# S5's output matrices scaled later, and the experts' routing weights taken earlier

## The chip, the cores and the metric

The kernel runs on one NeuronCore of a Trainium2 chip, written directly against the engines: TensorE (PE), VectorE (DVE), ScalarE (ACT), GpSimd (POOL) and SyncE (SP) each have their own instruction stream, and they wait for each other by semaphores. The metric is the device time of one execution in microseconds (us). Before the change it is 2880.5 us, the median of three runs (2880.3 to 2881.02).

## The reference

One token sequence (256 tokens, width 1024, float32) goes through a first block and then through a second one of four layers.

```python
mod = silu(c) @ w_ada + b_ada                    # six modulation rows
h = x + gt1 * hybrid_mixer(modulate(rmsnorm(x), sh1, sc1))
h = h + gt2 * hier_moe(modulate(rmsnorm(h), sh2, sc2))

# hybrid_mixer: proj = a_in @ w_in, split into S5 (a linear recurrence with the
# output matrices c_re, c_im) and a gated delta rule; both joined by w_out
# S5: b_bar = ((lam_bar - 1) / lam) * b;  y = real(c . states) + d * u

# hier_moe: a token takes its best group of 4, and the best 2 of the group's 8 experts
w_k = softmax(top_val) * p_grp
out = sum over experts e of combine[:, e] * ((silu(hf @ wg[e]) * (hf @ wu[e])) @ wd[e])
```

The second block is attention or gated mixing between two feed-forward halves in each of four layers. The change doesn't touch it.

## The kernel before

Every large product is done in float32 by three matmuls of rounded parts: high times high, high times low, low times high. A weight slab of 128 x 2048 values is loaded by DMA, ACT copies it to its rounded high half (`slab_hi`, or `split_hi` in the first stages), and DVE subtracts to get the low half (`slab_lo`, `split_lo`). PE may use a slab once its low half stands. The order on each engine is written out by hand: each engine's function is a list of steps that run in just this order, so a step that waits holds everything behind it on that engine.

**The head.** PE multiplies eight slabs of `w_ada` (`ada_pe`, L1131), DVE takes each result out of PSUM (`ada_dve`, L1145 and L1154). There are two PSUM banks, so PE may begin slab j when slab j-2 has been taken out. GpSimd builds the tables of S5's rotations meanwhile, and DVE helps with the last two levels (`s5_table_dve`). `s5_c_dve` (L1273 to L1278) scales S5's output matrices `cx_re` and `cx_nim`, six operations of 128 x 512; it folds the factor (lam_bar - 1) / lam of the reference into c. It stands behind slab 0. PE needs its result only in `s5_pe`.

**The projections.** `w_in_pe`, `w_in_act` and `w_in_dve` work through ten slabs of `w_in`. ACT evacuates projection j and copies slab j+2's high half; DVE makes slab j+2's low half (L348) and, for j from 2 to 7, applies the convolution (L1344, L1346).

**The experts.** Tokens are sorted into five blocks of 128 slots: blocks 0, 1 and 2 for the groups in the order of their load, 3 and 4 for the largest one. The masks `mask(t, b)` pick tokens. `gather_pe` (L1838) brings a block's rows into PSUM with 32 matmul records, in two halves. `block_dve` modulates them (L1996), `block_hi_act` rounds them (L1949), and DVE makes their low half (L2001). There are 40 passes, one for an expert and a block. In pass n PE does `gate_up_pe` for the first half of the inner dimension, turns the hidden values of pass n-1 (`turn_h_pe`, L1880), does the second half, and then `down_pe` for pass n-1. Each half of `gate_up` and each `down` is a group of twelve 128 x 512 matmuls (L406 to L408). Two things are put into the first passes: `slot_weights_pe` (L1847), which brings the routing weights to the slots, and `turn_masks_pe` (L1856), which transposes the masks for the way back. `turn_masks_pe` waits until all five blocks have left PSUM; ACT copies the result (L1979, L1980), and `down_pe` of pass 3, the first that accumulates in the banks used for it, waits for these copies. The weights themselves are 21 small DVE steps (L2024 to L2083) with one exponential on ACT (L1962).

## Time and profile before

| | |
|---|---|
| median of 3 runs | 2880.5 us |
| profiled execution | 2873.54 us, span 2871.7 us |
| PE busy | 2752.7 us (96%) |
| DVE, ACT, POOL busy | 1597.9 (56%), 1233.0 (43%), 140.9 us (5%) |
| mean granted PE clock | 0.98 of full |
| HBM read | 506.04 MB, 177 GB/s over the span |

PE is busy for nearly the whole span, but a PE that is busy on a lower clock counts as busy too. So its idle times and the granted clock have to be read for single stretches. Times in rows are in us from the start of the span. A timeline row gives start, length, engine, line, operation, the count of merged instructions, and in brackets the idle time before it with what ended it. A name that ends in q is an engine's queue of issued DMAs. A float32 matmul of the modulation slabs shows as two records in the profile and one in the program's order, and so do the transposes and gathers.

### The profile page before, as it was taken

The numbers are of one execution on the slowest core, as the hardware profiler recorded it, in microseconds if no ns is written. First come the engines' busy times: TensorE is split into PE (matmuls) and PEld (weight loads), VectorE is DVE, ScalarE is ACT, GpSimd is POOL, SyncE is SP. The second block draws the span as 40 slices with busy tenths as digits, with TensorE's granted clock in tenths as the row PEclk, the third lists the DMA queues.
The fourth block names the chain that finished last, engine by engine and source line by source line (L and its number), as shares of the span: only waits on it lengthen the run. The fifth ranks groups of instructions, "written<-read, shape, count | busy, mean of one in ns | idle before, by whom it ended". The sixth has DMA issues, their size and how long they took to land. (4 is left out here: it accounts for less than half of the span.)

```text
span 2871.7 us, 35302 instructions
## 1 busy us (share of the span) xinstructions
PE 2752.7 (96%) x14506; PEld 2308.8 (80%) x14506; DVE 1597.9 (56%) x1821; ACT 1233.0 (43%) x1588; POOL 140.9 (5%) x227
## 2 busy tenths in 40 slices
PE   7988979999999999999998999999999999999998
PEld 6977877888788887888887888888878888896887
DVE  5884467767644536445455645545454464544544
ACT  3202245656534445344344434434453443444443
POOL 4000000000000100001000000000000010010000
PEclk9998989999999999999999999999999999999999
DMA  7432056878655544656553755554435556452652
GB/s 249 156 108 88 30 200 229 310 279 297 220 181 176 167 138 136 207 189 213 193 166 107 240 182 176 191 187 153 144 118 183 195 178 206 155 169 90 225 176 88
DMA packets 349485, 509.35 MB, mean 177 GB/s; under 512 B 14880, under 2 KB 295488, under 8 KB 349328
## 3 DMA queue, kind: packets, MB, share of 16 engines
q1 hardware_dynamic: 342960, 484.17, 49.9%
q0 software_dynamic: 5792, 20.78, 2.1%
q8 instruction: 112, 1.84, 0.3%
q10 hardware_dynamic: 576, 2.20, 0.2%
q14 instruction: 45, 0.37, 0.0%
HBM read 506.04 MB, written 1.05 MB: 177 GB/s over the span
## 5 line engine op out<-in xcount | busy, mean ns | idle before, releaser
L393 DVE TENSOR_TENSOR raw_r<-raw,whi 128x2048 fp32r<-128x2048 f32 x185 | 421.9, 2290 | 170.3 <-ACT whi L385 169.3
L833 ACT ACTIVATE h_hi<-psum 128x256 fp32r<-128x256 f32 x216 | 82.8, 383 | 758.5 <-PE psum L772 684.2
L385 ACT ACTIVATE whi<-raw 128x2048 fp32r<-128x2048 f32 x185 | 351.1, 1909 | 12.4 <-DMA raw<-in_w_up 6.7
L888 DVE TENSOR_TENSOR h_lo<-psum,h_hi 128x256 fp32r<-128x256 f32 x216 | 91.5, 424 | 437.1 <-ACT h_hi L833 437.1
L407 PE MATMUL psum<-place_lo,act_hi 128*128 128x512 f32 (+1 forms) x840 | 318.6, 379 | 0.0
L406 PE MATMUL psum<-whi,act_hi 128*128 128x512 f32 (+1 forms) x872 | 308.2, 353 | 5.4 <-DVE act_lo L639 4.3
L408 PE MATMUL psum<-whi,act_lo 128*128 128x512 f32 (+1 forms) x872 | 302.1, 346 | 0.0
L393 DVE TENSOR_TENSOR place_lo<-arena,place_hi 128x2048 fp32r<-128x2048 f32 x107 | 244.2, 2289 | 91.8 <-ACT place_hi L385 91.8
L407 PE MATMUL psum<-raw_r,act_hi 128*128 128x512 f32 (+1 forms) x808 | 283.8, 351 | 0.0
L406 PE MATMUL psum<-place_hi,act_hi 128*128 128x512 f32 (+1 forms) x592 | 234.1, 395 | 0.0
L408 PE MATMUL psum<-place_hi,act_lo 128*128 128x512 f32 (+1 forms) x592 | 228.6, 386 | 0.0
L406 PE MATMUL psum<-wlo,act_hi 128*128 128x512 f32 (+1 forms) x520 | 192.4, 370 | 13.4 <-DVE act_lo L639 9.5
L385 ACT ACTIVATE place_hi<-arena 128x2048 fp32r<-128x2048 f32 x107 | 202.9, 1908 | 1.3 <-DMA arena<-in_ff_w_in 1.3
L408 PE MATMUL psum<-wlo,act_lo 128*128 128x512 f32 (+1 forms) x520 | 187.4, 360 | 0.0
L406 PEld LDWEIGHTS psum<-whi,act_hi 128*128 128x128 f32 x872 | 165.7, 190 | 24.7 <-issue 4.8
L408 PEld LDWEIGHTS psum<-whi,act_lo 128*128 128x128 f32 x872 | 165.7, 190 | 21.0
L407 PEld LDWEIGHTS psum<-place_lo,act_hi 128*128 128x128 f32 x840 | 158.0, 188 | 29.1
L393 DVE TENSOR_TENSOR wlo<-wlo_f,wlo 128x2048 fp32r<-128x2048 f32 x61 | 139.7, 2290 | 73.2 <-ACT wlo L385 72.3
L407 PEld LDWEIGHTS psum<-raw_r,act_hi 128*128 128x128 f32 x808 | 153.7, 190 | 18.5
L826 ACT ACTIVATE scratch<-psum 128x256 f32<-128x256 f32 x216 | 82.1, 380 | 188.2 <-PE psum L408 188.2
L406 PE MATMUL psum<-act_hi,whi 128*128 128x256 f32 x496 | 142.4, 287 | 8.1 <-DVE act_lo L601 5.9
L407 PE MATMUL psum<-raw_r,h_hi 128*128 128x512 f32 x372 | 145.4, 391 | 0.0
(537 smaller groups left out, 5832.7 us busy)
## 6 DMA issues: line engine op xcount, KB each, us to landing
arena<-in_ff_w_in SPq DMA_DIRECT2D x182, 512.0 KB, 4.9
raw<-in_ff_w_in SPq DMA_DIRECT2D x126, 512.0 KB, 4.9
arena<-in_ff_w_out SPq DMA_DIRECT2D x88, 512.0 KB, 4.5
raw<-in_ff_w_out SPq DMA_DIRECT2D x68, 512.0 KB, 4.5
wlo_f<-in_ff_w_in SPq DMA_DIRECT2D x44, 512.0 KB, 4.9
raw<-in_w_ada SPq DMA_DIRECT2D x20, 1024.0 KB, 5.2
raw<-in_w_gate SPq DMA_DIRECT2D x35, 512.0 KB, 4.4
raw<-in_w_up SPq DMA_DIRECT2D x35, 512.0 KB, 5.4
```

The costliest lines, as they stand in the source:

```text
L385: act.activation(hi, loaded, ACT.Copy).then_inc(S("slab_hi"), 1)
L393: dve.tensor_tensor(lo, loaded, hi.bitcast(F32), ALU.subtract).then_inc(S("slab_lo"), 1)
L406: pe.matmul(out_ap, lhs[0], rhs[0], start=first, stop=False)
L407: pe.matmul(out_ap, lhs[0], rhs[1], start=False, stop=False)
L408: return pe.matmul(out_ap, lhs[1], rhs[0], start=False, stop=last)
L826: act.activation(pair_of(sil, g), gate_up(g)[:, 0:256], ACT.Silu).then_inc(S("pass_sil"), 1)
L833: act.activation(pair_of(turned_h[0], g), gate_up(g)[:, 0:256], ACT.Copy).then_inc(S("pass_turned_hi"), 1)
L888: dve.tensor_tensor(pair_of(turned_h[1], g), gate_up(g)[:, 0:256], pair_of(turned_h[0], g).bitcast(F32), ALU.subtract)\
```

## The change

Three steps are moved; no arithmetic is added or taken away.

1. `s5_c_dve` leaves the place behind modulation slab 0 and stands in `w_in_dve` behind the low half made at j = 1, which is that of the fourth slab (index 3). The counts of its semaphore change places with those of the tables.
2. The routing weights: `slot_weights_pe` moves ahead of the third gather and of the second half of pass 0. On DVE the weights' steps move ahead of block 0's low halves and of the first two expert slabs; `block_dve` is cut so that its two halves stand between them. On ACT the pair's exponential and the change to SiLU's table move ahead of block 0.
3. `turn_masks_pe` and ACT's copies of its result move from pass 3 to pass 4.

```diff
-S5_DVE = {..., "s5_c": (11,), "table_im": (12, 13),
+S5_DVE = {..., "table_im": (11, 12), "s5_c": (13,),
...
             for j in range(10):
                 next_lo(dve, "w_in", j, 10)
+                if j == 1:
+                    s5_c_dve(dve, done)
...
                 if n:
                     turn_h_pe(pe, n - 1)
+                if n == 0:
+                    slot_weights_pe(pe)
                 if n < 3:
                     gather_pe(pe, n + 2)
-                elif n == 3:
+                elif n == 4:
                     turn_masks_pe(pe)
                 gate_up_pe(pe, n, 1)
                 if n:
                     down_pe(pe, n - 1)
-                else:
-                    slot_weights_pe(pe)
...
             act.activation(gexp, gexp, ACT.Exp).then_inc(S("group_exp"), 1)
+            act.wait_ge(S("pair_diff"), 1)
+            act.activation(pair_e, pair_e, ACT.Exp).then_inc(S("pair_exp"), 1)
+            act.activation(warm, warm, ACT.Silu)
             block_hi_act(act, 0)
             slab_hi(act, "moe", 0)
             slab_hi(act, "moe", 1)
-            act.wait_ge(S("pair_diff"), 1)
-            act.activation(pair_e, pair_e, ACT.Exp).then_inc(S("pair_exp"), 1)
-            act.activation(warm, warm, ACT.Silu)
...
-                if n == 3:
+                if n == 4:
                     act.wait_ge(S("moe_turned_raw"), 1)
...
-            block_dve(dve, 0)
-            slab_lo(dve, "moe", 0)
-            slab_lo(dve, "moe", 1)
...
             dve.tensor_tensor(pair_e, m2, m1, ALU.subtract).then_inc(S("pair_diff"), 1)
+            block_dve(dve, 0, 0)
             dve.wait_ge(S("group_exp"), 1)
             done(dve.reduce_sum(gden, by(gexp, 4), AX))
             done(dve.reciprocal(gden, gden))
+            block_dve(dve, 0, 1)
             dve.wait_ge(S("pair_exp"), 1)
...
             dve.tensor_tensor(oh1, oh1, oh2, ALU.add).then_inc(S("moe_weights"), 1)
+            block_lo_dve(dve, 0)
+            slab_lo(dve, "moe", 0)
+            slab_lo(dve, "moe", 1)
             dve.wait_ge(S("moe_slot_raw"), 1)
...
                 if n < 4:
-                    block_dve(dve, n + 1)
+                    block_dve(dve, n + 1, 0)
+                    block_dve(dve, n + 1, 1)
+                    block_lo_dve(dve, n + 1)
...
                 ada_dve(dve, done, j)
-                if j == 0:
-                    s5_c_dve(dve, done)
-                elif j in (2, 4):
+                if j in (2, 4):
                     s5_table_dve(dve, done, TABLE_SHARED + j // 2 - 1)
```

In the orders below `arena`, `scratch`, `small` and `diag` are SBUF tiles and `cols` holds the matrices c. This is DVE's order in the projections before: the low halves of slabs 2, 3 and 4, and the first convolution.

```order
L1331 MEMSET scratch 128x2x3 x2
L348 TENSOR_TENSOR wlo<-raw,whi 128x2048 x3
L1344 TENSOR_SCALAR arena<-scratch,cols 128x256 x2
L1346 SCALAR_TENSOR_TENSOR arena<-scratch,cols,arena 128x256 x6
L348 TENSOR_TENSOR wlo<-raw,whi 128x2048
```

And this is the same place now.

```order
L1331 MEMSET scratch 128x2x3 x2
L348 TENSOR_TENSOR wlo<-raw,whi 128x2048 x2
L1273 TENSOR_TENSOR arena<-cols,small 128x512
L1274 TENSOR_TENSOR arena<-cols,small 128x512
L1275 TENSOR_TENSOR cols<-cols,small 128x512
L1276 TENSOR_TENSOR cols<-cols,small 128x512
L1277 TENSOR_TENSOR cols<-cols,arena 128x512
L1278 SCALAR_TENSOR_TENSOR cols<-cols,arena 128x512
L348 TENSOR_TENSOR wlo<-raw,whi 128x2048
L1346 TENSOR_SCALAR arena<-scratch,cols 128x256 x2
L1348 SCALAR_TENSOR_TENSOR arena<-scratch,cols,arena 128x256 x6
```

The six operations now stand between the low halves of slab 3 and slab 4.

DVE's order at the start of the experts before: the last masks, block 0, the first two expert slabs (L393), and only then the weights, of which the first two steps and the last one are shown with what follows them.

```order
L2063 TENSOR_SCALAR scratch<-arena,small 128x128 x4
L1996 TENSOR_SCALAR act_f<-psum,modc 128x128 x8
L2001 TENSOR_TENSOR blocks_r<-act_f,blocks_r 128x512 x2
L393 TENSOR_TENSOR raw_r<-raw,whi 128x2048 x2
L2024 TENSOR_REDUCE small<-small 128x2
L2025 TENSOR_TENSOR small<-small 128x16
...
L2083 TENSOR_TENSOR small<-small 128x16
L2085 COPY small<-psum 128x40
L393 TENSOR_TENSOR raw_r<-raw,whi 128x2048
```

Now, from the last of the first twelve steps of the weights on:

```order
L2072 TENSOR_TENSOR small<-small 128x2
L1996 TENSOR_SCALAR act_f<-psum,modc 128x128 x4
L2075 TENSOR_REDUCE small<-small 128x2
L2076 RECIPROCAL small<-small 128x2
L1996 TENSOR_SCALAR act_f<-psum,modc 128x128 x4
L2079 TENSOR_SCALAR small<-small 128x2
...
L2085 TENSOR_TENSOR small<-small 128x16
L2004 TENSOR_TENSOR blocks_r<-act_f,blocks_r 128x512 x2
L393 TENSOR_TENSOR raw_r<-raw,whi 128x2048 x2
L2090 COPY small<-psum 128x40
L393 TENSOR_TENSOR raw_r<-raw,whi 128x2048
```

All steps of the weights now stand ahead of the first slabs, and the copy of the slots' weights out of PSUM stands behind the first two slabs as it did.

PE's order in pass 0 before, from the last matmul of the first half on: the gather, the second half, the slots' weights.

```order
L408 MATMUL psum<-whi,blocks_r 128x512
L1838 MATMUL psum<-diag,arena 128x128 x16
L406 MATMUL psum<-whi,blocks_r 128x512
...
L408 MATMUL psum<-whi,blocks_r 128x512
L1847 MATMUL psum<-small,scratch 128x8 x8
L1847 MATMUL psum<-small,diag 128x8 x2
L406 MATMUL psum<-whi,blocks_r 128x512
```

Now:

```order
L408 MATMUL psum<-whi,blocks_r 128x512
L1849 MATMUL psum<-small,scratch 128x8 x8
L1849 MATMUL psum<-small,diag 128x8 x2
L1840 MATMUL psum<-diag,arena 128x128 x16
L406 MATMUL psum<-whi,blocks_r 128x512
```

The ten small matmuls have moved ahead of the gather and of the twelve matmuls of the second half. The ten mask transposes (L1856, now L1858) have moved by one pass, behind the turn of pass 3's hidden values.

## Rows read from the trace of the kernel before

**Rows 1.** Windows: length, busy PE, PEld, DVE, ACT, POOL, granted clock, DMA share, GB/s.

```profile
460.00:740.00 280.00, 280.00 (x1242) 226.42 (x1241) 206.30 (x147) 170.90 (x146) 0.00 (x0) 1.00 0.82 295
27.00:29.00 2.00, 2.00 (x6) 1.60 (x5) 1.97 (x3) 0.00 (x0) 1.40 (x1) 0.54 1.09 365
```

**Rows 2.** Waits of PE, whole kernel: us in total, times, longest.

```profile
PE psum L406 <- DVE raw_r L393: 5.8, 2, 3.2
...
PE psum L1856 <- DVE act_f L1996: 5.7, 1, 5.7
```

**Rows 3.** Timeline of PE, 0 to 48 us: start, length, what, idle before.

```profile
9.49 13.41 PE L1131 MATMUL psum<-raw,small 128*128 128x256 f32 x48 [9.49 <-DMA raw<-in_w_ada]
25.30 5.38 PE L1131 MATMUL psum<-act_f,small 128*128 128x256 f32 x16 [2.40 <-DVE diag L1145]
...
40.88 3.62 PE L1131 MATMUL psum<-raw,small 128*128 128x256 f32 x16
```

**Rows 4.** Timeline of DVE, 18 to 25 us.

```profile
19.40 1.10 DVE L1274 TENSOR_TENSOR arena<-cols,small 128x512 f32<-128x512 f32 x1
```

**Rows 5.** Issue of the eighth modulation slab, on the SP queue.

```profile
23.91 1.18 SPq L1116 DMA_DIRECT2D raw<-in_w_ada  x1
```

**Rows 6.** DMA issued from 23.9 to 25 us: KB, us to landing.

```profile
raw<-in_w_ada SPq DMA_DIRECT2D x1, 1024.0 KB, 11.8
```

**Rows 7.** Timeline of DVE, 60 to 125 us.

```profile
70.63 2.29 DVE L348 TENSOR_TENSOR wlo<-raw,whi 128x2048 fp32r<-128x2048 f32 x1 [3.47 <-ACT whi L343]
76.39 2.29 DVE L348 TENSOR_TENSOR wlo<-raw,whi 128x2048 fp32r<-128x2048 f32 x1 [3.47 <-ACT whi L343]
...
82.15 2.29 DVE L348 TENSOR_TENSOR wlo<-raw,whi 128x2048 fp32r<-128x2048 f32 x1 [0.19 <-ACT whi L343]
...
121.53 0.69 DVE L1415 TENSOR_TENSOR arena<-psum,arena 128x512 f32<-128x512 f32 x1 [2.53 <-PE psum L1375]
```

**Rows 8.** Timeline of ACT, 79 to 80 us.

```profile
79.72 0.60 ACT L1323 ACTIVATE scratch<-psum 128x512 f32<-128x512 f32 x1 [3.36 <-PE psum L408]
```

**Rows 9.** Timeline of DVE, 383 to 445 us.

```profile
383.81 1.37 DVE L1996 TENSOR_SCALAR act_f<-psum,modc 128x128 f32<-128x128 f32 x4 [2.31 <-PE psum L1838]
...
389.99 2.29 DVE L393 TENSOR_TENSOR raw_r<-raw,whi 128x2048 fp32r<-128x2048 f32 x1 [1.55 <-ACT whi L385]
...
404.02 0.20 DVE L2085 COPY small<-psum 128x40 f32<-128x40 f32 x1 [5.10 <-PE psum L1847]
...
412.62 0.47 DVE L2011 SCALAR_TENSOR_TENSOR scratch<-scratch,small,psum 128x256 f32<-128x256 f32 x1
...
441.00 0.42 DVE L888 TENSOR_TENSOR h_lo<-psum,h_hi 128x256 fp32r<-128x256 f32 x1
```

**Rows 10.** Timeline of PE, 395 to 470 us.

```profile
395.32 3.73 PE L1838 MATMUL psum<-diag,arena 128*128 128x128 f32 x32
...
401.69 1.85 PE L1847 MATMUL psum<-small,scratch 128*128 128x8 f32 x16
...
406.61 0.80 PE L406 MATMUL psum<-whi,blocks_r 128*128 128x512 f32 x1 [2.62 <-DVE raw_r L393]
...
413.14 0.44 PE L1880 MATMUL psum<-mats,scratch 128*128 128x128 f32 x2 [1.43 <-DVE scratch L2011]
...
444.02 1.97 PE L1856 MATMUL psum<-mats,scratch 128*128 128x128 f32 x8 [5.73 <-DVE act_f L1996]
...
464.33 0.38 PE L1880 MATMUL psum<-mats,scratch 128*128 128x128 f32 x2
```

**Rows 11.** Timeline of ACT, 397 to 448 us.

```profile
397.44 1.28 ACT L1963 ACT_TABLE_LOAD   x1
...
444.00 0.63 ACT L1949 ACTIVATE blocks_r<-act_f 128x512 fp32r<-128x512 f32 x1 [0.65 <-DVE act_f L1996]
446.46 1.02 ACT L1979 ACTIVATE turned_r<-psum 128x1024 fp32r<-128x1024 f32 x1 [1.82 <-PE psum L1856]
```

**Rows 12.** Page, costliest groups: busy, mean ns, idle before.

```profile
L385 ACT ACTIVATE whi<-raw 128x2048 fp32r<-128x2048 f32 x185 | 351.1, 1909 | 12.4 <-DMA raw<-in_w_up 6.7
```

More of the change, by code:

```diff
@@ L91 @@
 S5_ACT = {"c_act": (1,), "s5_step": (2,), "s5_rad": (3,), "s5_turn": (4, 5)}
-S5_DVE = {"half": (1,), "s5_lr": (2,), "s5_angle": (3,), "turn_pow": (4, 5, 6, 7, 8, 9, 10), "s5_c": (11,), "table_im": (12, 13),
+S5_DVE = {"half": (1,), "s5_lr": (2,), "s5_angle": (3,), "turn_pow": (4, 5, 6, 7, 8, 9, 10), "table_im": (11, 12), "s5_c": (13,),
           "s5_last": (14, 15, 16, 17)}
@@ L1988, in moe_act, with block_dve, block_lo_dve @@
             slab_hi(act, "ff0a", FF_HEAD[1])
-        def block_dve(dve, q):
-            b = BLOCK_ORDER[q]
-            for half in range(2):
-                dve.wait_ge(S("moe_gathered"), 2 * q + half + 1)
-                for c in range(4):
-                    k = 4 * half + c
-                    last = dve.tensor_scalar(mod_part(q, half)[:, c * P:(c + 1) * P], gathered(q, half)[:, c * P:(c + 1) * P],
-                                             modc[:, 3, k:k + 1], modc[:, 2, k:k + 1], ALU.mult, ALU.add)
-                last.then_inc(S("moe_block_f"), 1)
+        def block_dve(dve, q, half):
+            dve.wait_ge(S("moe_gathered"), 2 * q + half + 1)
+            for c in range(4):
+                k = 4 * half + c
+                last = dve.tensor_scalar(mod_part(q, half)[:, c * P:(c + 1) * P], gathered(q, half)[:, c * P:(c + 1) * P],
+                                         modc[:, 3, k:k + 1], modc[:, 2, k:k + 1], ALU.mult, ALU.add)
+            last.then_inc(S("moe_block_f"), 1)
+        def block_lo_dve(dve, q):
+            b = BLOCK_ORDER[q]
             for half in range(2):
```

## The prediction

> **What bounds the kernel now.** I read the windows first. In the expert passes PE is busy for all of 280.00 us at full clock, while DVE is busy 206.30 and ACT 170.90 [rows 1]. So there nothing is gained by relieving DVE or ACT; only time in which PE stands still, or runs at its lower clock, can be won. The list of PE's waits comes next: it is short, and the change touches three places in it. Two waits on a low half of a slab come to 5.8 us and one on the blocks' rows to 5.7 us [rows 2]; the third, 2.40 us on DVE among the modulation slabs, is in PE's timeline [rows 3]. I then read the timelines of PE, DVE and ACT round each place, to see what was queued ahead of what ended the wait.
>
> **Part one, S5's output matrices (`s5_c_dve`).** Six DVE operations leave the place behind the first modulation slab. There they hold DVE while PE has finished the third slab (9.49 + 13.41 = 22.90) and waits for the second's evacuation until 25.30 [rows 3]. Behind the wait the fourth slab takes 5.38 us where the eighth takes 3.62 [rows 3], because the granted clock had fallen to its lower level: it averages 0.54 from 27 to 29 us [rows 1], 1.2 GHz for nearly all of it. Without the six, DVE evacuates at once. The gain is the wait, 2.40, plus the slow slab, 5.38 - 3.62 = 1.76: 4.2 us.
>
> Is something else late then? The eighth slab is issued at 23.91 [rows 5] and lands 11.8 us later [rows 6], at 35.7. PE wants it at 22.90 + 4 x 3.5 = 36.9 (3.5 is a slab's 3.62 less the drain of its last matmul, which overlaps the next slab). That leaves a second. DVE's two table parts and its evacuations fit between PE's slabs, since PE asks only for the evacuation of the slab before the last. What follows the eighth slab (the scaling of the rows, the first projection) hangs on PE's and DVE's end of it, and moves forward by the same 4.2.
>
> The six operations now stand behind the fourth projection slab's low half. That split starts at 70.63 and ends at 72.92; the next starts at 76.39 after 3.47 us idle [rows 7]. The six are 128x512 each. Their price from two sides: beside GpSimd's table operations one took 1.10 [rows 4], with the chain 6.0 us in all if each did; a 128x512 operation with GpSimd idle took 0.69 [rows 7], which with a drain behind every second comes to 4.0 us. GpSimd's timeline is empty from 60 to 110 us, so I take 4.0. DVE is then free at 76.9 in place of 76.39, and the fifth slab's low half is ready at 79.15. PE wants it when the fourth slab ends, which is when ACT evacuates it, at 79.72 [rows 8]. So 0.5 us of cover remains, cost nothing. From then on DVE's idle time before a split is 0.19 [rows 7], by which the lateness melts slab by slab. With 6.0 the low half would come at 81.2, 1.5 us late, once.
>
> By the Trainium skill ("SBUF — State Buffer", section "Who interferes with whom") a DVE instruction with two SBUF inputs contends with a GpSimd instruction that reads SBUF; that is these operations at their old place, and the trace agrees (1.10 against 0.69 [rows 4, 7]). By that rule the price at the new place is the lower one.
>
> **Part two, the routing weights.** Before, DVE runs 21 small steps for the weights behind the first two expert slabs' splits, PE does its small products for them (`slot_weights_pe`) last in pass 0, at 401.69, and DVE waits 5.10 us for them until 404.02 [rows 9, 10] before it may split the second expert's first slab. PE then stands still 2.62 us until 406.61 and again 1.43 us until 413.14 [rows 10], and its matmuls between these are the slow ones. The change puts the small products ahead of the third gather: PE reaches them at 395.32 [rows 10], if the weights are ready. DVE's wait ends 401.69 - 395.32 = 6.37 us sooner. From there to the end of pass 0's hidden values (412.62) DVE has no wait [rows 9], so that whole run moves by 6.37. ACT must follow: its splits of the second expert's two slabs no longer stand behind the pair's exponential, and the slabs are loaded early. PE: gather and second half end near 404.0, the next half is ready for it, 2.8 us at full clock ends at 406.8, and the turn of pass 0 waits until 406.8 in place of 413.14. Gain 6.4 us. DVE bounds the rounds of passes 1 and 2, which keep their length.
>
> Are the weights ready at 395.32? The 21 steps take 4.2 us. They now fill DVE's idle stretches: 2.31 ahead of the first half block, 0.51 between its halves, 1.55 ahead of the first slab's low half at 389.99 [rows 9], 4.4 us together. They end at about 388.5, seven us early, and the first slab's low half is not late. On ACT a table load of 1.28 us [rows 11] moves ahead of the first block's copy; it starts at 384.1, when the pair's difference is there, and ends with the copy of one element at 385.6, where the half block is ready at 385.2 [rows 9]. 0.4 us late, behind which ACT waits for a DMA until 388.05 anyway. Cost nothing.
>
> The Trainium skill ("ScalarE: Activation LUTs", section "What ACT_TABLE_LOAD costs") speaks against this: 2.66 us for each switch of set, a drain of about 1.38 included. The row shows 1.28 and the next instruction right behind [rows 11]. By the rule the two half-block copies would end near 388.2 and the first slab's split start 0.1 us late: the sum would be smaller by 0.1.
>
> **Part three, the masks' turn.** In pass 3 PE stands still 5.73 us, from 438.29, because turning the masks waits for all ten half blocks; the turn at 444.02 and the half pass behind it run on the lower clock [rows 10]. From 438.29 to the turn of pass 4's hidden values at 464.33 [rows 10] it is 26.0 us. Now the same stretch is, at 2.8 us for a group of twelve 128x512 matmuls (280.00 / 1242 = 0.225 us each [rows 1], and a little for the step between groups): half pass 2.8; the product down of pass 2 waits for its low half, ready at 441.42 [rows 9], so it starts at 3.2 and ends at 6.0; half pass 8.8; turn 9.1; ten mask turns at full clock 1.4, to 10.5; half pass 13.3. Then down of pass 3 needs ACT's copies of the turned masks. ACT's queue: second half block until 444.63 [rows 11], which is 6.3 in this count; SiLU 0.3; three slab copies of 1.9 [rows 12] and one of 0.3; mask copies 1.02 [rows 11] and 0.3: 13.9. PE waits 0.6, starts down at 14.0, ends 16.8, half pass 19.6. Gain 26.0 - 19.6 = 6.4 us. Then PE is bound by itself again [rows 1] and keeps the lead.
>
> **The sum.** 4.2 + 6.4 + 6.4 = 17.0 us. The profiled execution took 2873.54 us (span 2871.7), the median of the runs is 2880.5, 7 us more; the saved stretches are alike in both, so I take them off the median: 2863.5 us, 0.6% faster. Against the profiled execution it would be 2856.5.
>
> **The rivals.**
> 1. The projections pay: DVE's six operations take 6.0 us, the fifth slab is 1.5 us late. For it: DVE has 5.6 us of work in every 5.76 us there. Against: GpSimd idle. Time 2865.0.
> 2. The head gains nothing, since the modulation slabs are bound by their DMAs: the margin of the eighth slab is only a second, and the DMA engines are full there (share 1.09, 365 GB/s [rows 1]). Against: loads land in the order of their issue and at 365 GB/s a slab takes 2.9 us, so each earlier slab has landed at least that much earlier than the one behind it, while PE wants them 3.5 apart. Time 2880.5 - 12.8 = 2867.7.
> 3. The masks' gain is given back: in pass 4 ACT holds the copies of the masks behind two slab copies, each of which waits for its DMA; PE's product down of pass 3 waits for them. If these slabs land 6.4 us behind need, 2869.9. Against: their places are given free by pass 2 and pass 1, over ten us earlier.
> 4. Slower: the same mechanism without a bound. The wait for the masks now hangs on two loads where before it hung on DVE alone. It decides from the point where the two slabs are ready 17 us behind PE's need; at 25 us the price is 25 less 17.0, 2888.5. A slab of 1024 KB landed in 11.8 us even in the fullest stretch [rows 6], so I hold this for nearly excluded.
> 5. That the change doesn't do what it says (the order of the engines' instructions shows all three moves) or is undone by a later stage, 2880.5.
>
> **How the numbers follow.** Forecast 0.76, rival 1 0.06, 2 0.07, 3 0.06, 4 0.02, 5 0.03. The range reaches to 2869.5 above, to take in rivals 1 and 2 and part of 3, and to 2858 below, since PE may find more of its lower clock gone than I count. A measurement of this kernel tells 0.2%, 5.8 us, from no change: faster is the forecast and rivals 1 to 3, 0.95; same 0.03; slower 0.02.
>
> **What would show it.** PE's modulation slabs in one run from 9.5 to 40.3 us at full clock. DVE's split of the fifth projection slab at 76.9 and no wait of PE behind it. The small products of the slots at about 391 (all stages here 4.2 earlier), no wait of PE for `raw_r` behind them, and only one of the two 5.8 us left, the 3.2 in front of the first slab. No 5.7 us wait in pass 3, the mask turns in pass 4, and a wait under 1 us for ACT's copies. The forecast is wrong if the eighth slab's end has moved by less than 3 us, if PE waits in the projections, or if the turn of pass 4 comes later than 448.5.

## The result, and the profile after

The changed kernel took 2862.1 us (median of 4 runs, 2858.9 to 2866.8), the kernel before 2880.4 us (4 runs, 2878.0 to 2881.0). The ratio on record is 0.9947, with an interval of 0.9933 to 0.9961: faster by 0.53%, 11.2 to 19.3 us. It is an estimate of its own and not the quotient of the two medians, which is 0.9936. The forecast was 2863.5. The profiled execution of the changed kernel took 2859.13 us (span 2857.3), that of before 2873.54 (span 2871.7).

Read the new profile in the same order. First the windows, of the changed kernel: the head from 24 to 29 us, and the expert passes that the change touches (length, busy time of PE, PEld, DVE, ACT and POOL with instructions, granted clock, DMA share, GB/s):

```profile
24.00:29.00 5.00, 5.00 (x25) 4.41 (x24) 4.49 (x5) 0.00 (x0) 3.48 (x3) 1.00 1.10 356
380.00:452.00 72.00, 67.82 (x383) 57.13 (x382) 60.02 (x86) 42.53 (x42) 0.00 (x0) 1.00 0.71 258
```

The same windows in the kernel before:

```profile
24.00:29.00 5.00, 3.70 (x9) 3.00 (x10) 4.83 (x8) 0.00 (x0) 4.18 (x4) 0.66 1.09 355
380.00:452.00 72.00, 59.01 (x325) 51.03 (x326) 51.93 (x98) 32.64 (x34) 0.00 (x0) 0.88 0.56 205
```

The clock went from 0.66 to 1.00 in the head and from 0.88 to 1.00 in the passes, and PE is busy for 67.8 of 72 us instead of 59.0. Of PE's waits in [rows 2], one of the two on `raw_r` (now 3.3 us, once) and the one on `act_f` are gone.

PE in the head of the changed kernel, from the fourth slab (start, length, engine, line, operation, tiles, count, idle before and what ended it):

```profile
22.61 3.62 PE L1131 MATMUL psum<-act_f,small 128*128 128x256 f32 x16
26.06 3.62 PE L1131 MATMUL psum<-scratch,small 128*128 128x256 f32 x16
...
37.86 3.69 PE L1131 MATMUL psum<-raw,small 128*128 128x256 f32 x16 [1.28 <-DVE diag L1145]
43.20 1.94 PE L546 MATMUL psum<-mats,scratch 128*128 128x128 f32 x16 [1.66 <-DVE scratch L586]
```

Against [rows 3] the wait of 2.40 us ahead of the fourth slab and the slow slab are gone, as forecast. The 1.28 us ahead of the eighth slab are new, and it is DVE's evacuation that ends them, not a DMA. What DVE and GpSimd did then, first DVE, then GpSimd (POOL):

```profile
30.70 2.00 DVE L1245 TENSOR_TENSOR arena<-arena,gain_row 128x1024 f32<-128x1024 f32 x1
32.62 3.38 DVE L1246 TENSOR_TENSOR arena<-arena,gain_row 128x1024 f32<-128x1024 f32 x1
36.03 1.23 DVE L1247 TENSOR_TENSOR arena<-arena 128x1024 f32<-128x1024 f32 x1
37.29 0.42 DVE L1145 TENSOR_TENSOR diag<-psum,mats 128x256 f32<-128x256 f32 x1
31.69 3.22 POOL L1247 TENSOR_TENSOR arena<-arena 128x1024 f32<-128x1024 f32 x1
```

The same stretch of the kernel before, DVE and then GpSimd:

```profile
35.15 1.97 DVE L1245 TENSOR_TENSOR arena<-arena,gain_row 128x1024 f32<-128x1024 f32 x1
37.05 1.21 DVE L1246 TENSOR_TENSOR arena<-arena,gain_row 128x1024 f32<-128x1024 f32 x1
33.69 2.35 POOL L1247 TENSOR_TENSOR arena<-arena 128x1024 f32<-128x1024 f32 x1
```

Read what lies beside what. Before, GpSimd's last operation ended at 36.04, under the first of DVE's three, and the other two (the first of them is shown) took 1.2 us each. Now DVE's three begin 4.45 us earlier and GpSimd's only 2.00, so DVE's L1246, from 32.62 on, lies beside 2.3 of the 3.2 us of GpSimd's L1247 (until 34.91) and takes 3.38 in place of 1.21. The three take 6.6 us instead of 4.4, and PE waits for the evacuation queued behind them. The eighth slab's load was no longer far off either: issued at 24.20 and 11.8 us under way, it landed at 36.0, 0.4 us before PE would have started on it (two slabs, 6.9 us, behind 29.51). The forecast had a margin of a second.

In the projections of the changed kernel, the first and the last of the six operations behind the fourth slab's split, and the next split on DVE:

```profile
69.43 0.69 DVE L1273 TENSOR_TENSOR arena<-cols,small 128x512 f32<-128x512 f32 x1
72.70 0.69 DVE L1278 SCALAR_TENSOR_TENSOR cols<-cols,arena 128x512 f32<-128x512 f32 x1
73.30 2.28 DVE L348 TENSOR_TENSOR wlo<-raw,whi 128x2048 fp32r<-128x2048 f32 x1
```

The six cost 0.69 each and 3.9 us in all (69.43 to 73.30), and the low half is ready at 75.58. PE has no wait there.

PE in pass 0 of the changed kernel, from the first expert product to the turn of its hidden values; below it the DVE copy that waits for the small products:

```profile
388.49 0.47 PE L406 MATMUL psum<-whi,blocks_r 128*128 128x512 f32 x1 [3.33 <-DVE raw_r L393]
391.38 1.85 PE L1849 MATMUL psum<-small,scratch 128*128 128x8 f32 x16
393.52 3.82 PE L1840 MATMUL psum<-diag,arena 128*128 128x128 f32 x32
...
402.83 0.44 PE L1882 MATMUL psum<-mats,scratch 128*128 128x128 f32 x2
393.70 0.20 DVE L2090 COPY small<-psum 128x40 f32<-128x40 f32 x1 [2.75 <-PE psum L1849]
```

The two waits of 2.62 and 1.43 us in [rows 10] are gone, and DVE waits 2.75 us where it waited 5.10 [rows 9]. PE at the masks, now in pass 4, and the first of ACT's two copies of them, with the turn of pass 4's hidden values at 447.25 (it stood at 464.33 [rows 10]):

```profile
431.15 0.51 PE L406 MATMUL psum<-wlo,h_hi 128*128 128x512 f32 x1 [0.37 <-DVE h_lo L888]
437.07 1.03 PE L1858 MATMUL psum<-mats,scratch 128*128 128x128 f32 x8
441.60 0.47 PE L406 MATMUL psum<-act_hi,h_hi 128*128 128x512 f32 x1 [0.47 <-ACT turned_r L1982]
447.25 0.38 PE L1882 MATMUL psum<-mats,scratch 128*128 128x128 f32 x2
440.15 1.03 ACT L1981 ACTIVATE turned_r<-psum 128x1024 fp32r<-128x1024 f32 x1
```

Pass 3 has only the wait of 0.37 us that was forecast, eight of the ten mask turns take 1.03 us at full clock (1.97 before [rows 10]), and ACT's copies make PE wait 0.47.

The same points of the program in both traces, in us:

| point | before | after | lead |
|---|---|---|---|
| transposes of the weights begin (L546) | 46.15 | 43.20 | 2.95 |
| router's result copied on DVE | 374.74 | 370.63 | 4.11 |
| first expert product (L406) | 392.43 | 388.49 | 3.94 |
| turn of pass 0's hidden values | 413.14 | 402.83 | 10.31 |
| turn of pass 2's | 437.85 | 427.54 | 10.31 |
| turn of pass 4's | 464.33 | 447.25 | 17.08 |
| end of the span | 2871.7 | 2857.3 | 14.4 |

### The profile page after: what moved, and what is told of

Read it like the earlier page. It is cut to its first block and busy times, and to the rows that moved or that the text cites. A ratio compares the mean times of both kernels' runs of the same rounds, so it can differ in the third digit from the quotient of the medians.

```text
span 2857.3 us, 35303 instructions
## 1 busy us (share of the span) xinstructions
PE 2749.0 (96%) x14506; PEld 2305.6 (81%) x14506; DVE 1597.7 (56%) x1821; ACT 1233.5 (43%) x1588; POOL 138.2 (5%) x227
## 5 line engine op out<-in xcount | busy, mean ns | idle before, releaser
L393 DVE TENSOR_TENSOR raw_r<-raw,whi 128x2048 fp32r<-128x2048 f32 x185 | 421.8, 2290 | 168.0 <-ACT whi L385 167.2
L406 PE MATMUL psum<-whi,act_hi 128*128 128x512 f32 (+1 forms) x872 | 308.7, 354 | 5.4 <-DVE act_lo L639 4.3
L393 DVE TENSOR_TENSOR place_lo<-arena,place_hi 128x2048 fp32r<-128x2048 f32 x107 | 244.2, 2290 | 90.7 <-ACT place_hi L385 90.7
L406 PE MATMUL psum<-place_hi,act_hi 128*128 128x512 f32 (+1 forms) x592 | 234.1, 395 | 0.0
L406 PE MATMUL psum<-wlo,act_hi 128*128 128x512 f32 (+1 forms) x520 | 192.5, 370 | 13.4 <-DVE act_lo L639 9.5
L406 PEld LDWEIGHTS psum<-whi,act_hi 128*128 128x128 f32 x872 | 166.4, 191 | 24.8 <-issue 4.8
L393 DVE TENSOR_TENSOR wlo<-wlo_f,wlo 128x2048 fp32r<-128x2048 f32 x61 | 139.7, 2290 | 74.4 <-ACT wlo L385 73.7
L406 PE MATMUL psum<-act_hi,whi 128*128 128x256 f32 x496 | 142.1, 286 | 8.1 <-DVE act_lo L601 5.9
```

Source lines behind the costliest of these rows:

```text
L393: dve.tensor_tensor(lo, loaded, hi.bitcast(F32), ALU.subtract).then_inc(S("slab_lo"), 1)
L406: pe.matmul(out_ap, lhs[0], rhs[0], start=first, stop=False)
```

## Experiments

Lengths between near points of this table are used below, since they hang less on what happened earlier in a run than times from its start do. Each experiment's kernel, the changed one and the one before had one execution profiled; two kernels were profiled a second time, as experiments of their own. The ratios below compare with runs of the kernel before from the same batch, whose medians were 2879.8, 2878.9 and 2881.9 us. In the largest batch, 24 runs of the kernel before, single runs took 2871.5 to 2886.1 us.

**The first part alone.** The kernel before with `s5_c_dve` at its new place.

```
- if j == 0: s5_c_dve(dve, done)          # behind the first modulation slab
- elif j in (2, 4): s5_table_dve(...)
+ if j in (2, 4): s5_table_dve(...)
+ if j == 1: s5_c_dve(dve, done)          # in the loop over the projection slabs
```

> Part one alone: the scaling of S5's output matrices behind the fourth projection slab, the rest as before. Theory (the parts add): in the trace the end of the eighth modulation slab comes 3 us earlier than before, the router's first copy on DVE about 4 us earlier, the turns of passes 0 and 4 keep their distance from it; time 2877 us, 0.1% faster. Rival (the head's gain is lost in the projections or in the S5 stage): the router's first copy within 1 us of 374.7. Either way DVE's second table part beside GpSimd makes PE wait about 1.3 us ahead of the eighth slab.

Measured: 2871.7 us, ratio 0.9979 (0.9967 to 0.9992). The transposes begin at 43.12, 3.0 us earlier than before, with the same new wait on PE:

```profile
37.77 3.69 PE L1131 MATMUL psum<-raw,small 128*128 128x256 f32 x16 [1.48 <-DVE diag L1145]
```

The new wait stands by itself, without the other parts. The size of the gain is less firm than one pair says. The head with its old order was profiled in two more kernels, those of the second and of the third part alone. PE's fourth slab, in the first and then in the second of them:

```profile
25.85 5.38 PE L1131 MATMUL psum<-act_f,small 128*128 128x256 f32 x16 [3.16 <-DVE diag L1145]
26.80 5.38 PE L1131 MATMUL psum<-act_f,small 128*128 128x256 f32 x16 [3.62 <-DVE diag L1145]
```

The wait that was 2.40 us in the kernel before is 3.16 and 3.62 there, and the transposes begin at 46.69 and 47.64 instead of 46.15. With the new order they begin at 42.96 to 43.53 in seven profiled executions, and the new wait is 0.62 to 1.48. So the move brings 2.6 to 4.7 us, by which old head and which new one are compared; 3.0 is the pair of the first two profiles. Two more readings differ from what was expected. The router's result comes 5.7 us earlier than before, not 4, as the stretch from the transposes to it took 2.7 us less. And the turn of pass 0 lies 40.2 us behind it, not 38.4, since PE ran at its low clock behind the first expert product.

**The second part alone.** The kernel before with the weights and the small products at their new places.

```
- else: slot_weights_pe(pe)               # last in pass 0
+ if n == 0: slot_weights_pe(pe)          # ahead of the gather
  (with ACT's pair exponential and DVE's weight steps as in the change)
```

> Part two alone: the routing weights early, the masks turned in pass 3 and the S5 scaling in its old place. Theory (the slots' weights end a wait of DVE): DVE's wait for the slots' weights ends 6.4 us earlier than before, measured from the router's first copy (22.9 us behind it in place of 29.3), and so does the turn of pass 0 (32.0 in place of 38.4); PE waits once, not twice, for a low half; time 2874 us. Rival (the granted clock, not the wait, carries the gain, and it depends on what else the stage does): the turn of pass 0 gains less than 5 us.

Measured: 2872.7 us, ratio 0.998 (0.9968 to 0.9992). From the first expert product to the turn of pass 0 it takes 15.90 us, against 20.71 before and 14.34 in the changed kernel. The gain of 4.8 us (4.5 from the router's copy on, 38.4 before and 33.9 now) is under the 5 us that the rival named. But PE waits once for a low half and not twice, as the theory said, and the missing 1.56 us are clock, not order: PE's window behind the first product, of this kernel and then of the changed one, differs in the column of the granted clock:

```profile
388.00:402.00 14.00, 11.50 (x70) 10.39 (x71) 9.27 (x6) 5.76 (x4) 0.00 (x0) 0.88 0.88 355
```
```profile
386.00:400.00 14.00, 11.51 (x77) 10.45 (x78) 10.85 (x11) 6.01 (x5) 0.00 (x0) 1.00 0.89 356
```

The same two lengths come in the other kernels. With the small products ahead of the gather the stretch took 14.3 in four profiled executions and 15.9 in five; with them at the old place 20.7 in two and 22.27 in the one of the first part alone (clock 0.88 from 386 to 400 us). Within one clock the gain is 20.71 - 14.34 = 6.37 and 22.27 - 15.90 = 6.37: the forecast's term to the digit. So the rival is right that the clock moves the length, by 1.56 us from one execution to another, and wrong that it carries the gain.

**The third part alone.** The kernel before with the masks' turn in pass 4.

```
- elif n == 3: turn_masks_pe(pe)
+ elif n == 4: turn_masks_pe(pe)
- if n == 3: act.wait_ge(S("moe_turned_raw"), 1) ...
+ if n == 4: act.wait_ge(S("moe_turned_raw"), 1) ...
```

> Part three alone: the masks turned in pass 4. Theory: from the turn of pass 2 to the turn of pass 4 it takes 19.7 us in place of 26.5, as in the changed kernel; the start of the experts is as before; time 2873.6 us. Rival (the gain needs the lead in loads that part two gives): ACT's copies of slabs in pass 4 wait for DMAs, the distance is over 22 us and the time above 2876.

Measured: 2870.7 us, ratio 0.9976 (0.996 to 0.9992). From the turn of pass 2 to that of pass 4 it takes 19.67 us, in the changed kernel 19.71 and before 26.48. In its new place the turn makes the stretch 19.4 to 19.7 us long in every profile but one (18.75, see below). The old order's 26.48 is less steady. With the first part alone the stretch took 25.68, with the second alone 27.00, and the cause can be read: the wait ends 6.17 us behind the turn of pass 2 in all three, but the low clock behind it lasts for 2, 6 and 8 of the expert matmuls (0.54 us and more each, where 0.40 is full clock). So the part brings 6.8 us against the kernel before, and 6.0 to 7.3 by how long PE stays at the low clock there. No slab copy of ACT waited for a DMA, so the gain doesn't need the second part's lead. The three ratios alone give 0.21, 0.20 and 0.24%, 0.65% together, where the whole has 0.53% and, measured again below, 0.56%. The parts add up within what the intervals leave open.

**The small products behind the gather.** The changed kernel with its first part and third part whole, and the small products one place later.

```
+ if n < 3: gather_pe(pe, n + 2)
  if n == 0: slot_weights_pe(pe)
- if n < 3: gather_pe(pe, n + 2)
```

> The changed kernel, but PE's small products for the slots' weights stand behind the third gather instead of ahead of it, so half of the move is undone. Theory (DVE's run behind the slots' weights bounds the start, so the gain is what PE does behind them): the gather's 3.5 us come back in full at the turn of pass 0 (35.5 us behind the router's first copy in place of 32.2), time 3.5 us above the changed kernel. Rival (PE bounds the run by now): less than 1.5 us comes back.

Measured: 2868.1 us, ratio 0.9954 (0.9936 to 0.9972). From the first product to the turn of pass 0 it takes 19.44 us, 5.1 more than in the changed kernel. PE shows the gather's 3.6 us ahead of the small products, and the half pass behind them partly at 0.63 us for a matmul where full clock gives 0.40:

```profile
397.12 3.73 PE L1840 MATMUL psum<-diag,arena 128*128 128x128 f32 x32
400.69 1.85 PE L1849 MATMUL psum<-small,scratch 128*128 128x8 f32 x16
404.75 0.63 PE L406 MATMUL psum<-whi,blocks_r 128*128 128x512 f32 x1
412.14 0.44 PE L1882 MATMUL psum<-mats,scratch 128*128 128x128 f32 x2 [1.89 <-DVE scratch L2016]
```

Against the runs that have the same low clock behind the first product (15.90) the stretch is 3.54 us longer, one gather. So DVE's wait for the small products is what the run of pass 0 hangs on: moved by a gather, it moves by a gather. The rest of the 5.1, 1.56, is clock.

**Three more operations in the projections.** The changed kernel with three 128x512 operations on DVE behind the six.

```
  if j == 1:
      s5_c_dve(dve, done)
+     for _ in range(3): done(dve.tensor_tensor(arena[128x512], mats, mats, ALU.add))
```

> The changed kernel with three more DVE operations of 128x512 behind S5's six in the projections (work that nothing needs), 2.1 us in all. Theory (the place has 0.7 us of cover: in the changed kernel the fifth slab's low half ends at 75.58, PE wants it at 76.31): the fifth slab's low half is 1.4 us late, PE waits 1.4 us once, ahead of the fifth slab, and the later slabs wait for nothing or for little. Rival (the lateness is paid anew at each slab, since DVE has only 0.2 us to spare in each): PE waits in total over 3 us in the projections.

Measured: 2862.7 us, one run. ACT's evacuations of the projections show the price, and that it is paid once: the distance is 5.76 us up to the evacuation at 76.26, 7.63 to the next, and 5.76 again from there on (89.65); the last line is PE's wait:

```profile
76.26 0.60 ACT L1323 ACTIVATE scratch<-psum 128x512 f32<-128x512 f32 x1 [3.36 <-PE psum L408]
83.89 0.60 ACT L1323 ACTIVATE scratch<-psum 128x512 f32<-128x512 f32 x1 [5.23 <-PE psum L408]
77.84 0.38 PE L406 MATMUL psum<-act_hi,whi 128*128 128x256 f32 x1 [1.62 <-DVE wlo L348]
```

The three take 2.13 us and PE waits 1.62 (1.4 was expected), so by the wait 0.5 us of cover was left, the forecast's figure. ACT's next evacuation comes 1.87 late. Of the 0.25 between, 0.16 is the end of a matmul that the next one otherwise overlaps, and 0.09 the slower first matmul behind the wait (0.38 in place of 0.28 us). Past the edge only the difference is paid, once. A single run's time can't show 1.9 us; the trace does.

**The masks back in pass 3, with the wait filled.** The changed kernel with the masks' turn at its old place, and matmuls of no use ahead of it, so that PE is busy while it waits. First with 44 of them.

```
- elif n == 4: turn_masks_pe(pe)
+ elif n == 3:
+     keep_clock(pe, 5, 44)      # second kernel: 24
+     turn_masks_pe(pe)
```

> The changed kernel with the masks' turn back in pass 3, and 44 small matmuls of the unit matrix into a free bank in front of it, which fill PE's wait of 5.7 us. It splits the 6.8 us of the masks' part into wait and clock. Theory (most of it is the wait, a third the clock): PE stays at full clock through the stretch, the ten mask turns take 1.2 us in place of 2.4 and the half pass behind them 2.8 in place of 3.9, so that from the turn of pass 2 to the turn of pass 4 it takes 24.2 us, between 26.5 (masks in pass 3) and 19.7 (in pass 4). Rival (the slow clock is all of it, PE would have waited later anyway): under 21.5 us.

The filler was mis-sized. The 44 matmuls took 9.8 us, 0.22 each, longer than the wait of 5.73 that they were to fill, and the stretch from the turn of pass 2 to that of pass 4 was 28.17 us, which neither theory had. So it was run again with 24.

> The masks' turns back in the pass where they were, with 24 matmuls of no use (their results are not read) ahead of them instead of the 44 that had overshot: at 0.22 us each they take about 5.3 us, less than the wait of 5.7 us that stood there. My theory: the mask turns' gain of 6.8 us has two parts, the wait of about 4.5 and 2.2 from the half-speed clock that the wait brings; with the wait filled the clock stays at full speed and the stretch from the turn of pass 2 to that of pass 4 takes about 24.2 us (before 26.5, changed kernel 19.7). Rival: the wait is all of it, and the clock took nothing; then the stretch takes 26 us or more.

Measured: 24.30 us for the stretch. PE, with the filler, what is left of the wait, and the mask turns at full clock:

```profile
427.26 0.44 PE L1882 MATMUL psum<-mats,scratch 128*128 128x128 f32 x2
427.54 5.52 PE L539 MATMUL psum<-mats 128*128 128x128 f32 x48
433.43 1.09 PE L1858 MATMUL psum<-mats,scratch 128*128 128x128 f32 x8 [0.37 <-DVE act_f L1997]
...
451.56 0.38 PE L1882 MATMUL psum<-mats,scratch 128*128 128x128 f32 x2
```

The mask turns begin at the same point as before (6.17 us behind the turn of pass 2 in both), so nothing but the clock differs between 26.48 and 24.30. The gain of the third part against the kernel before is therefore 2.2 us of clock and 4.6 of waiting. Against the other two profiles of the old order the clock's share is 1.4 and 2.7 us (25.68 and 27.00); the waiting is the same.

**DVE's second table part one slab later.** The changed kernel, to see whether the new wait in the head is the operations that lie beside GpSimd's.

```
- if j in (2, 4): s5_table_dve(dve, done, TABLE_SHARED + j // 2 - 1)
+ if j in (2, 5): s5_table_dve(dve, done, TABLE_SHARED + (j == 5))
```

> The changed kernel with DVE's second table part one modulation slab later, behind the sixth. It tests what held the head's gain at 3 us where 4.2 were forecast. Theory (DVE's operation ran beside GpSimd's last table operation, 3.38 us in place of 1.21, and made the sixth slab's evacuation late): GpSimd is through when DVE's large operations begin or nearly so, none takes over 2.1 us, PE waits for no evacuation, and the transposes behind the modulation start at 41.9 in place of 43.2. Rival (the eighth slab's load is what PE really waits for): they start at 43.0 or later, whatever DVE does.

Measured: 2859.1 us, ratio 0.9928 (0.9913 to 0.9943). The first two of DVE's three operations, GpSimd's last one, and PE:

```profile
34.23 1.22 DVE L1245 TENSOR_TENSOR arena<-arena,gain_row 128x1024 f32<-128x1024 f32 x1
35.37 1.22 DVE L1246 TENSOR_TENSOR arena<-arena,gain_row 128x1024 f32<-128x1024 f32 x1
31.68 2.36 POOL L1247 TENSOR_TENSOR arena<-arena 128x1024 f32<-128x1024 f32 x1
36.49 3.62 PE L1131 MATMUL psum<-raw,small 128*128 128x256 f32 x16
41.76 1.94 PE L546 MATMUL psum<-mats,scratch 128*128 128x128 f32 x16 [1.65 <-DVE scratch L586]
```

GpSimd is done at 34.04, before DVE begins, and DVE's three take 3.6 us instead of 6.6. PE's wait is gone and the transposes begin at 41.76, 1.44 us earlier than in the changed kernel and 4.4 earlier than in the kernel before: as much as the term that the forecast had. The rival, that PE really waits for the eighth slab's load, is out: they begin well before 43.0 with that load where it was. The Trainium skill ("SBUF — State Buffer", section "Who interferes with whom") says that a DVE instruction with two inputs in SBUF contends with a GpSimd instruction that reads SBUF; it gives no size for it. The trace agrees, and here the size is 2.2 us on one operation of 1.2.

**The changed kernel once more**, beside that one.

> The changed kernel once more, for its time and for a second trace. Theory (the 2.4 us by which the lead shrinks behind the experts, in code that the change does not touch, come from stretches of lower clock that fall where they will): here the lead of the trace over the trace of before at the end of the experts and at the end of the span differ by another amount than 2.4, with other places of lower clock; ratio of the timed runs 0.994. Rival (the change costs something later): the lead shrinks by 2 to 3 us again, at the same places (the second layer's start at 1100 and the third's at 1545).

Measured: 2863.1 us, ratio 0.9944 (0.993 to 0.9958). The parts repeat: transposes at 42.96, from the turn of pass 2 to that of pass 4 19.69 us. The lead at the end of the span is only 7.3 us this time, at the turn of pass 4 11.7. Against the first profile of the same kernel it lacks 5.4 us before that turn: 4.0 between the transposes and the router's copy (331.45 us in place of 327.43) and 1.56 of low clock in pass 0. Behind the turn it loses 4.4 against the kernel before, in code that the change doesn't touch. The amount is another than in the first profile (2.7), as the theory said, but the sign is the same; more on this at the end of the next section.

**Both mends**, and the one with the table part again. The second edit puts ACT's copies of the masks ahead of its slab copy in pass 4.

```
  if n == 4:
      act.wait_ge(S("moe_turned_raw"), 1) ...            # the two mask copies
+ if fresh: slab_hi(act, "moe", SLAB_OF[PASSES[n + 1][0], 1])
- (the slab copy ahead of them)
```

> The changed kernel with two places mended that its trace showed: VectorE's second part of S5's table behind the fifth slab of the projections' preparation instead of the fourth, and ScalarE's two copies of the turned masks ahead of its copy of the next pass's slab in the pass before the last. My theory: TensorE's wait of 1.3 us for the last diagonal scaling in the head is gone (transposes of the weights at about 41.8 us of the span instead of 43.2), and TensorE's wait of 0.47 us for the first turned slab in the turns stays at most 0.2; from the turn of pass 2 to that of pass 4 19.3 us instead of 19.7. Together about 1.8 us against the changed kernel, a median near 2860. Rival: the mask copies are not what the wait of 0.47 us ends on, and moving them ahead delays the slab copy so that the first product of the next pass waits 0.4 to 1.0 us more: the turn of pass 4 then comes at 19.7 us or more, and only the head's 1.4 us remain.

> The kernel with the table's second part behind the fifth slab once more, beside the one with both edits. My theory: transposes of the weights at 41.8 us, from the turn of pass 2 to that of pass 4 19.7 us, and a median within 0.2% of the kernel with both edits, since the second edit is worth 0.4 us or less, which times can't tell. Rival: the first measurement (2859.1) was luck of the clock; then this one is as the changed kernel (2863.1) or above it, with the transposes still at 41.8.

Measured: both mends 2859.1 us, ratio 0.9933 (0.9919 to 0.9946); the table part alone 2861.0, ratio 0.9927 (0.9913 to 0.994). With both, the wait for the masks is gone (what is left is a short one on DVE), and the stretch from the turn of pass 2 to that of pass 4 takes 19.43 us, without the second edit 19.70 in this profile:

```profile
438.54 0.50 PE L406 MATMUL psum<-act_hi,h_hi 128*128 128x512 f32 x1 [0.17 <-DVE h_lo L888]
```

The transposes begin at 41.96 and 42.24. The first mend brings 0.7 to 1.4 us in the head in all three profiles that have it. The second takes away the wait it was aimed at, but its 0.3 us are not shown as a gain: the first profile of the kernel with the table part alone has 18.75 us for the same stretch, without that edit. There the low clock fell in pass 0's gather (0.51 from 397 to 400 us) and not ahead of the small products, so PE came late to work that DVE and ACT had ready, and waited only 0.22 us for the masks. In time, either kernel is faster than the kernel before by 0.7%. From the changed kernel (0.53 and 0.56%) they are not told apart with these few runs; the intervals overlap.

## Why the prediction was right

**The sum.** Forecast 17.0 us off the median; measured 18.3 between the medians, 11.2 to 19.3 by the interval, and 17.08 in the trace at the turn of pass 4. By terms:

| term | forecast | measured |
|---|---|---|
| head | 4.2 | 3.0, over all profiles 2.6 to 4.7 (4.4 with the table part one slab later) |
| projections | 0 | 0, with 0.5 us of cover |
| weights | 6.4 | 6.37 |
| masks | 6.4 | 6.8, over all profiles of the old order 6.0 to 7.3 |

That 17.08 comes so near to 17.0 is luck in part. The head, the weights and the masks make 2.95 + 6.37 + 6.77 = 16.1 us in this pair of profiles; the last 1.0 was gained between the transposes and the first expert product (the table's 2.95 and 3.94), in code that no term is about and whose length differs by up to 8 us from one profile to another. The agreement of the medians says no more than the interval does.

**The head: right in the mechanism, mis-sized.** The wait of 2.40 us and the low clock behind it went as forecast, and the DMAs kept up, though with 0.4 us to spare and not a second, so rival 2 was nearer than it looked. But PE's eight slabs did not run in one piece, and the eighth slab's end moved from 44.50 to 41.55, by 2.95 us. The prediction had said that it is wrong if that end moves by less than 3; by its own sign, and by a hair, it failed here. The step that failed is "DVE's two table parts and its evacuations fit between PE's slabs". That took the table parts at their durations of before. They had been short because GpSimd was through with its tables soon after the first of them began, and the move put DVE's second part 4.45 us earlier and beside GpSimd's last operation. So it took 6.6 us in place of 4.4, and PE waited 1.28 us for the evacuation behind it. The prediction used the rule on DVE and GpSimd for the operations that moved, and not for those that stayed and came to lie elsewhere. Putting the part where GpSimd is done brought the term back.

**The projections: right.** The six took 3.9 us (taken: 4.0), the cover of 0.5 us was there, and three more operations of 2.13 us together made PE wait 1.62, once. That is the shape of rival 1, which didn't happen.

**The weights: right in each step, at one and the same clock.** In five of the nine profiles that have the small products ahead of the gather the stretch is 1.5 to 1.6 us longer, by low clock that the prediction had no term for; the changed kernel's first profile happened to have none. The small products came at 391.38 (forecast "about 391"), DVE's steps for the weights were through at 384.4, and the table load cost nothing. On that load the prediction weighed the Trainium skill ("ScalarE: Activation LUTs", section "What ACT_TABLE_LOAD costs"), by which a switch takes 2.66 us with the drain. At its new place the load took 1.28 and no drain shows, neither between it and the activation ahead of it, which ended at 379.99, nor behind it:

```profile
380.01 1.28 ACT L1962 ACT_TABLE_LOAD   x1
381.30 0.20 ACT L1962 ACTIVATE small<-small 128x1 f32<-128x1 f32 x1
```

So here the measurement decides against the page's sum, as in [rows 11]; the load itself is as long as the page has it.

**The masks: right, 0.4 too low.** The waits that were forecast in the new order, 0.4 us on the low half and 0.6 on ACT's copies, were 0.37 and 0.47. The 0.4 lie in the mask turns. Up to them the count fits (9.1 us counted and 9.1 measured from the start of the stretch), but the ten took 1.0 us, from 437.07 to 438.08, where the count had 1.4. The experiment with the filler adds what the sum didn't separate: about a third of the gain is clock (2.2 of 6.8; 1.4 to 2.7 by the profile of the old order). Rivals 3 and 4 didn't happen: ACT's two slab copies waited for no DMA.

**What isn't settled.** Of the lead of 17.1 us at the turn of pass 4 the span kept 14.4. The remaining 2410 us of the program took 2407.4 us before, 2410.1 after, and 2408.3 to 2411.8 in the other eleven profiles; the second part alone, with nothing else moved, has 2411.4. So the kernel before has the shortest of all thirteen. It was profiled once, in an execution of 2873.54 us that was itself 7 us under the median, so it may be a quick one by chance; a cost of the change of some 1 to 4 us in this stretch is not excluded by the traces. The stretch from the transposes to the router's copy took 328.6 before, 327.4 after, and 325.8 to 333.6 in the others. One place shows what differs, PE's window around 1085 us (around 1100 in the kernel before), the columns as above; changed kernel, kernel before, and the kernel with both mends:

```profile
1070.00:1095.00 25.00, 20.47 (x143) 16.70 (x142) 12.74 (x21) 15.49 (x35) 0.00 (x0) 0.93 0.30 94
```
```profile
1087.00:1112.00 25.00, 20.47 (x156) 16.58 (x153) 13.40 (x23) 15.81 (x35) 0.00 (x0) 1.00 0.29 89
```
```profile
1070.00:1095.00 25.00, 20.47 (x155) 16.70 (x155) 13.58 (x22) 15.80 (x35) 0.00 (x0) 1.00 0.30 95
```

PE is busy for the same time, at another granted clock. The changed kernel's second profile has 0.93 there again. But the kernel with both mends moves everything that the changed one moves and has full clock there, and so has the one with three more operations (1.00). So the low clock at that place doesn't follow from the change as such; whether it hangs on where in time a stage falls, or on chance, these runs don't tell. Either way these differences, up to 8 us from one profiled execution to another in code that is alike, are larger than any of the three terms, and the terms could be read only because each was taken between near points of the program. Even there the same code differs from profile to profile, by up to 1.5 us in the head, 1.6 in the stretch of the weights and 1.3 in that of the masks.

## What to carry to other kernels

When a step leaves a queue, list what moves up in its place and what the engines beside it do at that time: an operation that was cheap where it stood can be dear a few us earlier, and the queue behind it pays. Size each part between two near points of the trace, over a pass or less, and not by the ends of the span, where unchanged code differs by more than the part. And read the same stretch in more than one profile, since the low clock behind one and the same wait lasted for 2, 6 or 8 matmuls here. Where a wait brings PE's low clock behind it, count both: here they were 4.6 and 1.4 to 2.7 us in one place, 2.40 and 1.76 in another.

## What the runs showed of the hardware that was not expected

- A DVE operation of two SBUF inputs, 128x1024, took 1.21 us with GpSimd through with its tables, 1.97 beside the end of GpSimd's L1247, and 3.38 beside most of it. GpSimd's operation took 3.22 us in that case instead of 2.35, so both lose.
- PE's matmuls of the half pass that begins with the first expert product ran partly at the low clock in six of thirteen profiles (six to eight of them at up to 0.63 us instead of 0.40); in a seventh the low clock fell in the gather behind them. It made the stretch to the turn of pass 0 longer by 1.5 to 1.6 us, with the weights at either place. In the seventh most of this was made good by the turn of pass 4.
- 24 fp32 matmuls of 128x128 by 128x128 (48 in the records, two for each), with operands that were ready, took 5.5 us and held the granted clock at 1.00 through a wait; without them it fell.
